# Moving conditioning groups and gate rows, and rebuilding the ends of the four sub-layers

## The reference

```
shift, scale, gate = split(silu(c) @ ada_w + ada_b)          # per sub-layer, from the conditioning vector c
h = x * (1 + scale) + shift
x = LayerNorm(alpha * x + (1 + gate) * f(h)) * ln_g + ln_b    # alpha = 4 ** 0.25
```

## Time and profile before

| | |
|---|---|
| time, three runs | 3009.69, 3012.66, 3017.41 us; median 3012.66 |
| the profiled execution | 3010.59 us, its span 3008.8 us |
| granted TensorE clock, mean | 0.96 of full speed |
| busy: TensorE | 2696.6 us, 90% (18304 matmuls) |
| busy: VectorE, ScalarE, GpSimd | 66%, 38%, 9% |
| chain that ended last | TensorE 75%, VectorE 9%, issue 9% |
| read from device memory | 632 MB, 211 GB/s over the span |

### The profile page before, as it was taken

How to read it: one execution, slowest core, us unless ns; L and a number is a source line. 1 busy time by engine, 2 the same in 40 slices (tenths; PEclk the granted TensorE clock), 3 DMA queues, 4 the chain that set the end, 5 groups by cost and what they waited for, 6 DMA issues and landing times.

```text
span 3008.8 us, 44267 instructions
## 1 busy us (share of the span) xinstructions
PE 2696.6 (90%) x18304; PEld 2245.6 (75%) x18304; DVE 1971.4 (66%) x1879; ACT 1140.1 (38%) x1268; POOL 258.4 (9%) x173
## 2 busy tenths in 40 slices
PE   1599978998698999999999689997879999999995
PEld 1488868997486888888888567775768888888884
DVE  7786655664675777777777677767464555555557
ACT  0233335554343333333333233337434333333332
POOL 0000000000004000000000056522012000000001
PEclk9999989998798999999999889999989999999998
DMA  9798840000284888788888358770436555555551
GB/s 353 267 377 297 327 184 10 15 7 4 94 312 154 307 307 312 297 317 306 318 299 302 123 218 298 280 278 1 168 127 208 191 186 194 184 192 191 186 194 70
DMA packets 256670, 636.25 MB, mean 211 GB/s; under 512 B 10190, under 2 KB 17028, under 8 KB 234148
## 3 DMA queue, kind: packets, MB, share of 16 engines
q1 hardware_dynamic: 250386, 621.77, 57.7%
q10 hardware_dynamic: 6162, 12.72, 1.1%
HBM read 632.35 MB, written 2.10 MB: 211 GB/s over the span
## 4 chain that ended last, share of the span: by engine, by line
PE 75%; DVE 9%; issue 9%; POOLq 2%; POOL 1%; DMA 1%; ACT 1%; DVEq 1%; SPq 0%; ACTq 0%
PE pa L541 12%; PE pa L542 12%; PE pa L543 12%; PE pb L541 5%; PE pb L543 5%; PE pb L542 5%; PE py L541 5%; PE py L543 5%; PE py L542 5%; DVE s_wl L448 2%; PE pt L2019 2%; PE pa L2019 2%; PE pb L2019 2%; DVE s_wide L487 1%; PE py L2019 1%
## 5 line engine op out<-in xcount | busy, mean ns | idle before, releaser
L448 DVE TENSOR_TENSOR s_wl<-s_raw,s_wh 128x2048 fp32r<-128x2048 f32 (+1 forms) x396 | 931.2, 2353 | 664.8 <-ACT s_wh L443 662.6
L443 ACT ACTIVATE s_wh<-s_raw 128x2048 fp32r<-128x2048 f32 (+1 forms) x396 | 758.2, 1915 | 1283.3 <-PE pa L543 623.4
L541 PE MATMUL pa<-s_wh,s_hth 128*128 128x512 f32 (+1 forms) x1760 | 702.2, 399 | 26.6 <-DVE s_wl L448 15.6
L542 PE MATMUL pa<-s_wl,s_hth 128*128 128x512 f32 (+1 forms) x1760 | 693.4, 394 | 0.0
L543 PE MATMUL pa<-s_wh,s_htl 128*128 128x512 f32 (+1 forms) x1760 | 692.1, 393 | 0.0
L541 PEld LDWEIGHTS pa<-s_wh,s_hth 128*128 128x128 f32 x1760 | 336.4, 191 | 108.7 <-DVE s_wl L448 24.1
L543 PEld LDWEIGHTS pa<-s_wh,s_htl 128*128 128x128 f32 x1760 | 335.7, 191 | 71.2
L542 PEld LDWEIGHTS pa<-s_wl,s_hth 128*128 128x128 f32 x1760 | 336.0, 191 | 67.1
L487 DVE SCALAR_TENSOR_TENSOR s_wide<-s_adaw,s_silu_c,s_wide 128x2048 f32<-128x2048 f32 x150 | 366.3, 2442 | 3.2 <-DMA s_adaw<-in_ada_w 3.0
L541 PE MATMUL py<-s_wh,s_guh 128*128 128x512 f32 x704 | 277.3, 394 | 20.7 <-DVE s_ysum L905 18.2
L543 PE MATMUL py<-s_wh,s_gul 128*128 128x512 f32 x704 | 275.5, 391 | 0.0
(11 more groups left out here) (321 smaller groups left out, 2487.1 us busy)
## 6 DMA issues: line engine op xcount, KB each, us to landing
s_raw<-in_ffn_w_in SPq DMA_DIRECT2D x176, 1024.0 KB, 5.1
s_adaw<-in_ada_w SPq DMA_DIRECT2D x160, 1024.0 KB, 5.7
s_raw<-in_ffn_w_out SPq DMA_DIRECT2D x88, 1024.0 KB, 5.1
s_raw<-in_ab_w_in SPq DMA_DIRECT2D x48, 1024.0 KB, 7.7
s_raw<-in_diff_w_in SPq DMA_DIRECT2D x48, 1024.0 KB, 7.2
s_raw<-in_ada_w SPq DMA_DIRECT2D x32, 1024.0 KB, 7.7
s_raw<-in_ab_w_out SPq DMA_DIRECT2D x16, 1024.0 KB, 9.3
s_raw<-in_diff_w_out SPq DMA_DIRECT2D x16, 1024.0 KB, 5.1
```

Of the source, the lines that this page charges most:

```text
L443: act.activation(wh[:, s % 2, :, 0:width], raw[:, s, :, 0:width], ACT.Copy).then_inc(hi_done, 1)
L448: dve.tensor_tensor(wl[:, s % 2, :, 0:width], raw[:, s, :, 0:width], wh[:, s % 2, :, 0:width].bitcast(F32), ALU.subtract).then_inc(lo_done, 1)
L541: pe.matmul(o, a_hi, w_hi, start=start and k == 0, stop=False)
L542: pe.matmul(o, a_hi, w_lo, start=False, stop=False)
```

## The change

1. **Group 2** of the conditioning: its last 16 steps stood in ab_in's last two chunks (8 steps, four of them after the last `low` and before the lora work) and in out0 (8). Now two of them stand in each RWKV iteration, one after L1668's call (`first`), one after the moments; their loads follow ab_in's weights in SyncE's queue.
2. **Groups 8 and 9**: group 8's steps in diff_in run two units later. Group 9's leave diff_in for the first two steps of FFN1, whose loops are partly unrolled for it.
3. **Gate rows**: in FFN0's tail ScalarE copies all four behind the first `high`; in FFN1 they are now made late too, in the same way.
4. **Ends**: the last `end_block` by token tile; the root by a GpSimd pow (`end_norm`) for all four ends; half rows normalised between the groups of the turn; the two `low`s that stood ahead of the normalisation now stand between the groups of the turn.
5. **Turns**: groups alternate between the banks `py` and `pb`; VectorE scales the even block, ScalarE the odd one twice (once to `htmp`, once rounded to `hth`) and rounds the even one.
6. **Final**: VectorE alone, in eight fused operations on half rows; four writes.

The core of the diff:

```diff
-        IN_PARTS = {1: 0, 2: 4, 3: 8, 4: 12, 6: 16, 7: 20, 8: 24, 9: 28, 11: 32}
+        IN_PARTS = {1: 0, 2: 4, 3: 8, 4: 12, 6: 16, 7: 20, 8: 24, 9: 28}
...
         def turn_pe(pe, call):
             for g in range(KT // 2):
                 n = call * 8 + g
                 if n >= 2:
                     pe.wait_ge(h_scaled, n - 1)
+                    pe.wait_ge(h_hi, n - 1)
...
-                        mm = pe.transpose(py[:, g % 2, j * SEQ + i * P:j * SEQ + (i + 1) * P],
+                        mm = pe.transpose(turn_bank(g)[:, j, i * P:(i + 1) * P],
                                           xt[:, i, (2 * g + j) * P:(2 * g + j + 1) * P], ident)
...
         def turn_act(act, call):
+            shift = small[:, 16:32] if call else ada[:, 0, 0:16]
             for g in range(KT // 2):
                 n = call * 8 + g
+                k = 2 * g + 1
+                if g == 0:
+                    act.wait_ge(h_scaled, n + 1)
+                act.wait_ge(tr_done, n + 1)
+                if g >= 2:
+                    act.wait_ge(h_lo, n - 1)
+                src = turn_bank(g)[:, 1, 0:SEQ]
+                act.activation(htmp[:, g % 2, 1], src, ACT.Identity, scale=small[:, k:k + 1], bias=shift[:, k:k + 1])
+                act.activation(hth[:, k], src, ACT.Identity, scale=small[:, k:k + 1], bias=shift[:, k:k + 1])
                 act.wait_ge(h_scaled, n + 1)
-                act.activation(hth[:, 2 * g:2 * g + 2, :], htmp[:, g % 2], ACT.Copy).then_inc(h_hi, 1)
+                act.activation(hth[:, k - 1], htmp[:, g % 2, 0], ACT.Copy).then_inc(h_hi, 1)
...
+            def two_groups(g):
+                scaled(g)
+                scaled(g + 1)
+                lower(g)
+                lower(g + 1)
+            if call:
+                normal(0)
+            two_groups(0)
+            low(dve, c, 0)
+            if call:
+                normal(1)
+            two_groups(2)
+            low(dve, c, 1)
+            two_groups(4)
+            two_groups(6)
+            low(dve, c, 2)
+            low(dve, c, 3)
...
-                low(dve, c, 0)
-                low(dve, c, 1)
-            dve.wait_ge(end_rstd, n + 1)
-            for half in range(2):
...
+        def end_norm(pool, n):
+            pool.wait_ge(end_var, n + 1)
+            pool.tensor_tensor(small[:, 38:40], small[:, 34:36], small[:, 95:96].to_broadcast((P, NT)),
+                               ALU.pow).then_inc(end_rstd, 1)
...
-            dve.wait_ge(pa_free, 2 + 2 * (n0 + 4))
-            end_block(dve, n, 3)
+            for i in range(NT):
+                dve.wait_ge(pa_free, 2 + 2 * (n0 + 4) - 1 + i)
+                end_block(dve, n, 3, (i,))
...
             for q in range(1, 4):
                 high(act, c0 + 32, q)
-                if f == 0:
-                    gate_act(act, n, q - 1, late_gates[q - 1])
-            if f == 0:
-                gate_act(act, n, 3, late_gates[3])
+                if q == 1:
+                    for g in range(4):
+                        gate_act(act, n, g, late_gates[g])
...
+            if f:
+                step(1, 0, 0)
+                step(2, 0, 1)
+                with dve.Fori(3, FG) as g:
                     step(g)
...
-            for u in range(36, 42):
+            for u in range(32, 48):
                 load_part(sp, u, u % 2, parts[1, 1, u - 32])
...
+                if lev:
+                    cond_step(dve, 32 + 2 * t)
                 if front:
                     bonus(n)
...
                 if chain:
                     moments(c)
+                if lev:
+                    cond_step(dve, 33 + 2 * t)
...
-            for u in range(2, 48):
+            for u in range(4, 48):
                 low(dve, u // 4 + C_DIFF, u % 4)
-                if 2 <= u < 18:
-                    cond_step(dve, 126 + u)
+                if u < 20:
+                    cond_step(dve, 124 + u)
...
-                if 26 <= u < 42:
-                    cond_step(dve, 118 + u)
-            part_store(dve, 9)
...
+            def centred(i, half):
+                x, cols = xt[:, i, half * D // 2:(half + 1) * D // 2], slice(half * D // 2, (half + 1) * D // 2)
+                dve.scalar_tensor_tensor(x, x, small[:, 88 + 2 * i:89 + 2 * i], lng[:, cols], ALU.subtract, ALU.mult)
+            def finished(i, half):
+                x, cols = xt[:, i, half * D // 2:(half + 1) * D // 2], slice(half * D // 2, (half + 1) * D // 2)
+                dve.scalar_tensor_tensor(x, x, small[:, 38 + i:39 + i], lnb[:, cols], ALU.mult, ALU.add).then_inc(out_ready, 1)
```

More of the change, by code:

```diff
@@ L591, in factors_dve, with turn_dve, normal, scaled @@
                 dve.drain()
-        def turn_dve(dve, call):
+        def turn_dve(dve, call, c):
             shift = small[:, 16:32] if call else ada[:, 0, 0:16]
+            def normal(half):
+                if half == 0:
+                    dve.wait_ge(end_rstd, call)
+                cols = slice(half * D // 2, (half + 1) * D // 2)
+                for i in range(NT):
+                    ins = dve.tensor_scalar(xt[:, i, cols], xt[:, i, cols], small[:, 88 + 2 * i:89 + 2 * i],
+                                            small[:, 38 + i:39 + i], ALU.subtract, ALU.mult)
+                ins.then_inc(x_ready, 1)
+            def scaled(g):
+                k = 2 * g
+                dve.wait_ge(tr_done, call * 8 + g + 1)
+                if g >= 2:
+                    dve.wait_ge(h_lo, call * 8 + g - 1)
+                dve.tensor_scalar(htmp[:, g % 2, 0], turn_bank(g)[:, 0, 0:SEQ], small[:, k:k + 1], shift[:, k:k + 1],
+                                  ALU.mult, ALU.add).then_inc(h_scaled, 1)
             def lower(g):
@@ L827, in step @@
                     load_unit(sp, g * 3 + (c0 - 1) + n // 4, n % 4, w_in[n // 4, bass.ds(g, 1), n % 4])
-                    if u0 is not None and n:
+                    if g <= 2 * groups and n:
                         part(g, n - 1)
@@ L831, in step @@
                     load_unit(sp, g * 3 + (c0 + 1), q, w_out[bass.ds(g - 1, 1), q])
-                    if u0 is not None and q == 2:
+                    if g <= 2 * groups and q == 2:
                         part(g, 7)
-            if u0 is not None:
-                for g in range(1, FG):
-                    step(g)
-            else:
-                with sp.Fori(1, FG) as g:
-                    step(g)
+            for g in range(1, FG):
+                step(g)
             for q in range(4):
@@ L849, in gate_up @@
                 high(act, c + 1, 0)
-                if first and f:
-                    gate_act(act, n, 0, py[:, 0])
                 if not (first and f == 0):
@@ L856, in gate_up @@
                 high(act, c + 1, 1)
-                if first and f:
-                    gate_act(act, n, 1, py[:, 1])
                 act.wait_ge(unit_done, c * 4 + 6)
@@ L914, in lower @@
                                   guh[:, 2:4].rearrange("p k t -> p (k t)").bitcast(F32), ALU.subtract).then_inc(gul_ready, 1)
-            for n in range(2, 8):
+            for n in range(4, 8):
                 low(dve, c0 + n // 4, n % 4)
@@ L956, in ffn_dve, with ffn_pe @@
                 end_block(dve, n_end, q - 1)
-            add(c0 + 32, 3, u0 + 43)
-            end_block(dve, n_end, 3)
-        def ffn_pe(pe, c0, f, u0, n, p0=None):
+            for i in range(NT):
+                add(c0 + 32, 3, u0 + 43, (i,))
+                end_block(dve, n_end, 3, (i,))
+        def ffn_pe(pe, c0, f, u0, n, p0):
             def turn(g):
@@ L974, in output @@
                     multiply(pe, c, q, (guh, gul), py, tile0=py_done, k0=0, free=(py_free, u + q))
-            project(pe, c0, n_of[f], (hth, htl), pa_done, pa_free, pa, call=n,
-                    between=lambda s: gate_pe(pe, n, s - 2, py[:, s % 2]) if f and s >= 2 else None)
-            project(pe, c0 + 1, f, (hth, htl), pb_done, pb_free, pb,
-                    between=lambda s: gate_pe(pe, n, s + 2, py[:, s % 2]) if f and s < 2 else None)
+            project(pe, c0, n_of[f], (hth, htl), pa_done, pa_free, pa, call=n)
+            project(pe, c0 + 1, f, (hth, htl), pb_done, pb_free, pb)
             turn(f)
@@ L987, in step @@
                 turn(g + f)
-            if p0 is None:
-                with pe.Fori(1, FG) as g:
+            if f:
+                step(1)
+                step(2)
+                part_cols(pe, p0 // 16)
+                with pe.Fori(3, FG) as g:
                     step(g)
@@ L1545, in _ @@
             factors_dve(dve, 0)
[L1546 to L1550 removed]
+            turn_dve(dve, 0, 0)
             for first in (1, 6):
```

151 lines of the change are left out of this document (54 added, 97 removed).

## The result

| | before | after |
|---|---|---|
| median of the runs | 3015.03 us | 3099.49 us |
| range | 3009.69 to 3017.42 | 3095.24 to 3102.75 |
| span of the profiled execution | 3008.8 | 3095.9 |
| granted clock, mean | 0.96 | 0.947 |

The ratio is 1.0288, with a 95% interval of 1.0272 to 1.0305. I had forecast 2988 us, range 2979 to 3000, and 0.03 for slower. The spans differ by 87.1 us.

A forecast was written before the change was run, and what follows sets the result against it. The prediction took TensorE, busy for 90% of the span, as the bound, so only its gaps counted. Its terms summed to −23.0 us: 2987.6 from 3010.59, 2989.7 from the median, given as 2988, range 2979 to 3000.

The forecast's parts named there:

- Group 8 moves two units later, into the rotation, where a unit took 6.6: +2.1: diff_in: group 8's steps move beside GpSimd's rotation, where a unit took 6.6 us; 2.1 us longer.
- my slower rival: RWKV pairs: group 2's steps lie on the chain, up to 4.7 us a pair, 33 for seven; 3019 us, chance 0.04.
- my signs of being wrong: Trace after: pairs longer by 1 us, a turn under 18 or over 21, fused operations off 1.15, diff_in units over 6.6.
- lora work earlier: End of ab_in: with group 2's steps gone, lora starts at about 432.1 instead of 435.0; 2.8 us saved.
- seven RWKV pairs: RWKV: group 2's steps fill VectorE's waits for TensorE; six pairs cost 0, the seventh 1.2 us.
- end 1, variance: FFN0's tail: gate copies behind the first `high` bring the variance 7.9 us earlier.
- a turn: Turn after an end: unit 0 starts 19.6 us after the variance, against 17.6 before; 2.0 us longer.
- GpSimd's pass, two units of diff_in: Early diff_in: the pass starts sooner with four two-input VectorE operations beside it, not six; 5.3 us saved.
- group 9 out of diff_in: diff_in: slow units return to 5.44 us and column matmuls go; 10.8 us saved.
- group 9 in FFN1: FFN1: a pair of steps with a group costs 4.9 us more, plus 0.8 behind a turn; 5.7 us longer.
- the final: Program's end: eight fused operations on VectorE alone, 1.15 us each; 13.95 us from last variance to end, 6.4 saved.
- The milder form of rival (a): RWKV pairs: VectorE waits for GpSimd's root beside the second step, 4.5 us in sum; 2992 us, chance 0.10.

The follow-up runs named there:

- experiment 2: Changed kernel with group 8's loads in diff_in issued one unit later: 3006.45 us, ratio 0.9979 to before.
- experiment 1: Changed kernel with group 8's loads in diff_in issued two units later, like VectorE's steps: 2986.78 us, ratio 0.9906 to before.
- experiment 9: repaired kernel with group 2's last sixteen steps back in ab_in's end and out0, none in the RWKV pairs: 2987.76 us, ratio 0.9925 to before.
- repaired kernel: Changed kernel with group 8's loads in diff_in issued two units later (the edit of experiment 1): 2986.78 us, ratio 0.9906 to before.
- experiment 8: repaired kernel with group 9 back in diff_in instead of FFN1: 2995.56 us, ratio 0.9947 to before.
- experiment 5: Kernel before with group 8's steps and loads both two units later in diff_in: 3011.85 us, ratio 1.0001 to before.

## Why the prediction was wrong, step by step

**The step that failed** is "Group 8 moves two units later, into the rotation, where a unit took 6.6: +2.1" in diff_in. I priced VectorE's steps by the units in which they would stand, and did not ask what waits for a step: `load_part` of part u waits until step u − 2 has run, and stands in SyncE's queue ahead of the next weights. The diff shows VectorE's line changed and SyncE's `if 2 <= u < 18` beside it unchanged. For group 2 I did look at SyncE's queue; for group 8 I did not. In its place the runs show a distance: with VectorE's step two units behind its old place, SyncE is one unit ahead instead of three, and a unit costs the ring of 14.4 us divided by the units in flight: 14.64, 7.27 with one more (experiment 2), and three would be 4.8, less than what TensorE needs, so the 6.08 of experiment 1 has another bound: TensorE's 5.44, and VectorE's 6.6 beside the rotation. The cost was 111.6 us in thirteen units. No rival of mine named it either; my slower rival put the danger into the RWKV pairs, where experiment 9 finds none. Of my signs of being wrong, units over 6.6 in diff_in came true by far; beside it only the fused operations were off, by a tenth of a microsecond.

The other steps, with what they measured:

| step | predicted | measured | where |
|---|---|---|---|
| lora work earlier | −2.8 | −2.9 | 430.82 against 434.91, less 1.24 gained before |
| seven RWKV pairs | +1.2 | +1.4 | from lora to out0's first unit |
| end 1, variance | −7.9 | −8.2 | 1706.47 against 1715.59, less 0.9 gained before |
| a turn | +2.0 | +1.6 | 19.18 against 17.58, end 1 |
| ends 0 and 2 with their turns | +0.2 each | −0.1 each | last unit before to first unit behind: 29.05 against 29.11, 28.72 against 28.79 |
| first turn | +1.1 | +0.4 | 124.86 against 124.47 |
| GpSimd's pass, two units of diff_in | −5.3 | −4.7 | 18.42 for 23.15, repaired kernel |
| group 8 under the rotation | +2.1 | +2.6 | repaired kernel, units 205 to 219 |
| group 9 out of diff_in | −10.8 | −10.2 to −12.3 | experiment 8 |
| group 9 in FFN1 | +5.7 | +4.2 to +8.2 | experiment 8 |
| FFN1's gates out of its first project | −3.6 | −3.4 | units 266 to 269 |
| gate matmuls before FFN1's last output | +1.3 | −0.6 or +0.8 | units 391 and 392: 15.36 against 16.01 before, 14.57 in experiment 5 |
| the final | −6.4 | −7.3 | 13.05 from 3082.85 to the span's end, against 20.36 |

With the missing edit made, the forecast change of −23.0 stands against −20.6 between the two spans (2988.2 and 3008.8) and −27.6 between the medians (2986.78 and 3014.35). Every term, in the repaired kernel that of group 8 too, came within some 2.5 us of its forecast. So the sizes were right in the main, and the sign was decided by the one row that was not read. That the sum comes out so near is in part luck, since single spans differ by several us through the clock (last section).

Two sizes of the final were off in opposite ways. The fused operation took 1.28 us, or 1.24 where two follow each other, just above my upper bound of 1.23. But from the last of them (3092.75) to the span's end are 3.1 us and not the 4.25 that I kept.

The two-pointer operation of ScalarE took 0.56. The 0.473 of the one-pointer row with the 93 ns that the Trainium skill ("ScalarE: Activation LUTs", "What ACT_TABLE_LOAD costs") gives for a further pointer makes an estimate of 0.57, and the trace agrees.

The milder form of rival (a) did not come, since it is GpSimd and not VectorE that waits in the pairs. Its root of 128x4 took 3.07 us instead of 1.01, beside the step that starts at 621.84, runs its usual 2.35 and leaves L1673 on time:

```profile
621.98 3.07 POOL L1118 TENSOR_TENSOR s_small<-s_small 128x4 f32<-128x4 f32 x1 [31.05 <-DVE s_small L1701]
```

In the final the root of 128x2 took 1.68 instead of 0.70, beside a fused operation that starts 0.16 us ahead of it:

```profile
3082.94 1.68 POOL L728 TENSOR_TENSOR s_small<-s_small 128x2 f32<-128x2 f32 x1 [717.48 <-DVE s_small L717]
```

The Trainium skill ("SBUF — State Buffer", "SBUF: two separate sides") says that of a GpSimd operation and a VectorE operation with two SBUF inputs the one that starts first keeps the shared ports for its whole length; both pairs of rows agree. It does not always spare VectorE: beside GpSimd's rotation in diff_in its operations grow from 2.3 to 3.4 us, and GpSimd's from 1.27 to between 3.2 and 3.4, as in this row of the kernel before:

```profile
1797.22 3.36 POOL L776 TENSOR_TENSOR s_qkv<-s_qkv,s_cst 128x512 f32<-128x512 f32 x1
```

## What to carry to other kernels

When a step moves in one engine's list, look for every wait on the semaphore that it raises and read what is queued behind each waiter: a load that waits for a consumer holds back all loads behind it. Count the distance, in units, between a queue's issue and the work that releases it; the time of a unit is at least the ring of issue, landing and processing divided by that distance, and a ring of 14 us that is free at three units costs 9 us a unit at one. Two engines that index the same sequence by their own loops have to be changed together.
